# Feed-forward nets of a decoder trunk: another order of the weight chunks, two pairs of banks, loops of two steps, and reordered ends

## The reference

```python
def swiglu(x, w_gate, w_up, w_down):
    return (jax.nn.silu(x @ w_gate) * (x @ w_up)) @ w_down
...
    for l in range(DEPTH):
        x = layer_norm(ALPHA * x + 0.5 * swiglu(x, ffn1_w_gate[l], ffn1_w_up[l], ffn1_w_down[l]), ln1_g[l], ln1_b[l])
        mix = hybrid_mixer(x, w_in[l], ...)
        x = layer_norm(ALPHA * x + mix, ln2_g[l], ln2_b[l])
        x = layer_norm(ALPHA * x + 0.5 * swiglu(x, ffn2_w_gate[l], ffn2_w_up[l], ffn2_w_down[l]), ln3_g[l], ln3_b[l])
    return x
```

## Time and profile before

| | |
|---|---|
| median of 3 runs | 1083.57 us (1083.33 to 1083.84) |
| the profiled execution's own time | 1083.67 us |
| its span, first to last instruction | 1081.9 us |
| granted TensorE clock, mean over the span | 0.999 of full speed |
| busy: TensorE, its weight loads, DVE, ACT, GpSimd | 1072.1, 882.7, 772.0, 579.4, 137.3 us |
| moved by DMA | 226.39 MB, 209 GB/s over the span |

### The profile page before, as it was taken

One profiled execution on the slowest core, in us unless ns is written; L12 is line 12 of the kernel. 1 busy time (PEld: TensorE's weight loads), 2 busy tenths in 40 slices (PEclk: granted clock), 3 DMA queues, 4 the chain that ended last, 5 costly groups with the idle time before them and its releaser, 6 DMA issues.

```text
span 1081.9 us, 14282 instructions
## 1 busy us (share of the span) xinstructions
PE 1072.1 (99%) x5197; PEld 882.7 (82%) x5197; DVE 772.0 (71%) x779; ACT 579.4 (54%) x641; POOL 137.3 (13%) x137
## 2 busy tenths in 40 slices
PE   8999999999999999999999999999999999999997
PEld 6888888888888788888888888888878887888886
DVE  5756557799979775555679665677999787655566
ACT  5755654768554544444456655547774546344441
POOL 1498000000000000000006970000000000000000
PEclk9999999999999999999999999999999999999999
DMA  8877879355566486777737877775455674688761
GB/s 285 263 216 231 296 223 225 105 184 171 175 185 208 149 272 226 233 259 225 250 124 231 248 244 254 230 199 165 148 166 157 195 268 133 209 268 270 235 208 40
DMA packets 192371, 226.39 MB, mean 209 GB/s; under 512 B 31540, under 2 KB 157128, under 8 KB 192328
## 3 DMA queue, kind: packets, MB, share of 16 engines
q1 hardware_dynamic: 192328, 225.83, 65.5%
HBM read 214.26 MB, written 11.53 MB: 209 GB/s over the span
## 4 chain that ended last, share of the span: by engine, by line
PE 97%; DMA 1%; SPq 1%; DVE 1%; issue 0%; ACT 0%; DVEq 0%
PE ps L578 25%; PE ps L555 19%; PE ps L557 18%; PE ps L556 18%; PE ps L538 4%; PE ps L540 2%; PE ps L974 1%; PE ps L976 1%; PE ps L975 1%; PE ps L593 1%; DMA raw<-in_ffn_w_up 1%; PE ps L901 1%; DMA tp<-in_ln_b 0%; PE ps L686 0%; PE ps L685 0%; PE ps L684 0%
## 5 line engine op out<-in xcount | busy, mean ns | idle before, releaser
L1449 DVE TENSOR_TENSOR w_lo<-raw,w_hi 128x2048 fp32r<-128x2048 f32 x172 | 399.9, 2329 | 166.7 <-ACT w_hi L1058 165.6
L1058 ACT CAST w_hi<-raw 128x2048 fp32r<-128x2048 f32 x172 | 328.1, 1910 | 162.1 <-PE ps L578 78.9
L555 PE MATMUL ps<-w_hi,xT 128*128 128x512 f32 x848 | 331.8, 391 | 0.3 <-DVE w_lo L1461 0.2
L556 PE MATMUL ps<-w_lo,xT 128*128 128x512 f32 x848 | 330.1, 389 | 0.0
L557 PE MATMUL ps<-w_hi,xT 128*128 128x512 f32 x848 | 330.1, 389 | 0.0
L555 PEld LDWEIGHTS ps<-w_hi,xT 128*128 128x128 f32 x848 | 159.2, 188 | 36.2 <-issue 2.5
L557 PEld LDWEIGHTS ps<-w_hi,xT 128*128 128x128 f32 x848 | 159.2, 188 | 33.0
L556 PEld LDWEIGHTS ps<-w_lo,xT 128*128 128x128 f32 x848 | 159.2, 188 | 32.7
L578 PE MATMUL ps<-w_hi,rows_hi 128*128 128x512 f32 x396 | 126.6, 393 | 0.0
L578 PE MATMUL ps<-w_hi,rows_lo 128*128 128x512 f32 x396 | 125.4, 390 | 0.0
L578 PE MATMUL ps<-w_lo,rows_hi 128*128 128x512 f32 x396 | 125.2, 389 | 0.0
(11 more groups left out here) (248 smaller groups left out, 1117.1 us busy)
## 6 DMA issues: line engine op xcount, KB each, us to landing
raw<-in_ffn_w_down SPq DMA_DIRECT2D x44, 1024.0 KB, 6.6
raw<-in_ffn_w_gate SPq DMA_DIRECT2D x86, 512.0 KB, 4.1
raw<-in_ffn_w_up SPq DMA_DIRECT2D x86, 512.0 KB, 5.2
raw<-in_w_in SPq DMA_DIRECT2D x30, 1024.0 KB, 5.1
hid_dram<-qT SPq DMA_DIRECT2D x160, 64.0 KB, 2.8
qT<-hid_dram SPq DMA_DIRECT2D x40, 256.0 KB, 2.6
raw<-in_w_out SPq DMA_DIRECT2D x8, 1024.0 KB, 4.9
raw<-in_w_in SPq DMA_DIRECT2D x8, 512.0 KB, 5.0
```

Source lines behind the costliest of these rows:

```text
L555: mm(o, xT[:, c, 0, tok], h, start=c == UPPER_FIRST[0], stop=False, skip_group_check=True)
L556: mm(o, xT[:, c, 0, tok], w, start=False, stop=False, skip_group_check=True)
L1058: nc.scalar.copy(w_hi[s][:, :], raw[s][:, :]).then_inc(hi_made.sem, 1)
L1449: tt(w_lo[s][:, :], raw[s][:, :], f32(w_hi[s][:, :]), ALU.subtract).then_inc(lo_made.sem, 1)
```

## The change

- The order of a step's chunks becomes upper, the down chunk, lower, on SP, ACT, DVE and TensorE alike. Chunk 4 is thus an upper chunk (two loads, gate and up) where it was a down chunk (one load), and the down chunks from then on come one place later in the stream. The last two chunks are down chunks in both orders.
- A step with an odd number puts gate and up into banks 6 and 7, one with an even number into 4 and 5. TensorE waits ahead of an upper chunk for the hidden of the step before last, and ahead of a lower chunk for the hidden of the last step.
- TensorE's, ACT's and DVE's loops hold two steps each and run three times; steps 2, 3 and 10 stand outside TensorE's loop. SP's loops still hold one step.
- At the end of a net ACT casts chunk 32 ahead of `hidden_hi` of step 9, and DVE makes the residual of chunk 32 behind `hidden` of the last step's first tile.
- The transposes of the norm vectors go to bank 3, and `vectors` stands ahead of the first step on DVE. In `last_steps` the three last down chunks change their buffers.

```diff
@@ load_ffn (SP)
-                load(l, k0 + 4, rows(w_down, l, 0))
+                load(l, k0 + 4, gate_up(w_gate, w_up, l, 1, 512))
                 small(1)
-                def step(i):
-                    load(l, k0 + i * 3 - 1, gate_up(w_gate, w_up, l, 1, i * 256), 2)
-                    turn_hidden(l, f * (STEPS - 1) + i - 1)
-                    load(l, k0 + i * 3, gate_up(w_gate, w_up, l, 0, i * 256), 0)
-                    load(l, k0 + i * 3 + 1, rows(w_down, l, i * 256 - 256), 1)
+                def step(n):
+                    load(l, k0 + n * 3 + 2, rows(w_down, l, n * 256 - 256), 2)
+                    turn_hidden(l, f * (STEPS - 1) + n)
+                    load(l, k0 + n * 3 + 3, gate_up(w_gate, w_up, l, 0, n * 256 + 256), 0)
+                def next_upper(n):
+                    load(l, k0 + n * 3 + 4, gate_up(w_gate, w_up, l, 1, n * 256 + 512), 1)
...
@@ ffn (TensorE)
-                def step(i):
-                    pe.wait_ge(h_made.sem, h_made.at(l, s0 + i))
-                    take(l, k0 + i * 3 - 1)
-                    half(2, 1)
-                    take(l, k0 + i * 3)
-                    return half(0, 0)
-                def down(i):
-                    take(l, k0 + i * 3 + 1)
-                    pe.wait_ge(h_lo.sem, h_lo.at(l, s0 + i))
+                def upper_half(i, bank):
+                    pe.wait_ge(h_made.sem, h_made.at(l, s0 + i - 1))
+                    take(l, k0 + i * 3 - 2)
+                    half(1, 1, bank)
+                def down(n, k):
+                    take(l, k)
+                    pe.wait_ge(h_lo.sem, h_lo.at(l, s0 + n))
+                def lower_half(i, bank):
+                    pe.wait_ge(h_made.sem, h_made.at(l, s0 + i))
+                    take(l, k0 + i * 3)
+                    return half(0, 0, bank)
+                def step(i, bank, start=False):
+                    upper_half(i, bank)
+                    down(i - 1, k0 + i * 3 - 1)
+                    accumulate(2, 0, start=start).then_inc(used.sem, 1)
+                    return lower_half(i, bank)
...
-                down(1)
-                accumulate(1, 0, start=True).then_inc(used.sem, 1)
-                with pe.Fori(2, STEPS - 2 if final else STEPS - 1) as i:
-                    step(i)
-                    down(i)
-                    accumulate(1, 0).then_inc(used.sem, 1)
+                step(2, 4, True)
+                step(3, 6)
+                with pe.Fori(2, STEPS // 2) as q:
+                    step(q * 2, 4)
+                    step(q * 2 + 1, 6)
...
@@ ffn (ACT), behind the loop
+                step(STEPS - 2, 6)
                 final = l == DEPTH - 1 and f == 1
+                split(l, k0 + FFN_CHUNKS - 2)
                 if final:
-                    split_tenth(k0 + FFN_CHUNKS - 2)
+                    split_eleventh(k0 + FFN_CHUNKS - 1)
                 else:
-                    split(l, k0 + FFN_CHUNKS - 2)
+                    split(l, k0 + FFN_CHUNKS - 1)
                 hidden_hi(l, b0 + STEPS - 1, final)
-                split(l, k0 + FFN_CHUNKS - 1)
                 silu(l, s0 + STEPS, (half_used.sem, half_used.at(l, f + 1)), 4, slice(0, 1))
...
@@ ffn (DVE), ahead of the first step
+                rest(l, k0 + 4)
+                if l == 0 and f == 0:
+                    vectors()
...
@@ ffn (DVE), behind the loop
+                step(STEPS - 2, 6)
                 if late:
                     late()
                 final = l == DEPTH - 1 and f == 1
+                rest(l, k0 + FFN_CHUNKS - 2)
+                hidden_lo(l, s0 + STEPS - 1, final)
+                hidden(l, s0 + STEPS, 4, slice(0, 1))
                 if final:
-                    rest_tenth(l, k0 + FFN_CHUNKS - 2)
+                    rest_eleventh(l, k0 + FFN_CHUNKS - 1)
                 else:
-                    rest(l, k0 + FFN_CHUNKS - 2)
-                hidden_lo(l, s0 + STEPS - 1, final)
-                rest(l, k0 + FFN_CHUNKS - 1)
-                hidden(l, s0 + STEPS, 4, slice(0, 1))
+                    rest(l, k0 + FFN_CHUNKS - 1)
```

More of the change, by code:

```diff
@@ L63 @@
 for _f in FFN0:
-    for _k in [_f, _f + 1] + [_f + 3 * _i - _n for _i in range(1, STEPS) for _n in (0, 1)]:
+    for _k in [_f, _f + 1, _f + 2, _f + 3] + [_f + 3 * _i - _n for _i in range(2, STEPS) for _n in (0, 2)]:
         DMAS[_k] = 2
@@ L671, in third_of_input, with last_steps @@
                         for c in (4 + 2 * part, 5 + 2 * part):
-                            last = gate_up(w_hi[2], w_lo[2], t, c, 4 + t)
+                            last = gate_up(w_hi[2], w_lo[2], t, c, 6 + t)
                 last.then_inc(used.sem, 1)
-            def last_steps(k0, s0, step, down, turn_hidden):
+            def last_steps(k0, s0, upper, down, lower, turn_hidden):
                 def products(t, at, left, right, start=False, stop=False, bank=None):
@@ L723, in ffn, with half @@
                     gate_up_by_token(l, f, norm)
-                def half(slot, upper):
+                def half(slot, upper, bank):
                     for t in range(NT):
                         for c in range(4 * upper, 4 * upper + 4):
-                            last = gate_up(w_hi[slot], w_lo[slot], t, c, 4 + t)
+                            last = gate_up(w_hi[slot], w_lo[slot], t, c, bank + t)
                         if t == 0:
@@ L1518, in ffn, with step, next_upper @@
                 rest(l, k0 + 3)
-                def step(i):
-                    rest(l, k0 + i * 3 + 1, 1)
-                    hidden_lo(l, s0 + i)
-                    rest(l, k0 + i * 3 + 2, 2)
-                    hidden(l, s0 + 1 + i)
-                    blocks_turned(l, s0 + 1 + i)
-                    rest(l, k0 + i * 3 + 3, 0)
-                step(1)
+                rest(l, k0 + 4)
+                if l == 0 and f == 0:
+                    vectors()
+                def step(n, bank):
+                    rest(l, k0 + n * 3 + 2, 2)
+                    hidden_lo(l, s0 + n)
+                    hidden(l, s0 + 1 + n, bank)
+                    blocks_turned(l, s0 + 1 + n)
+                    rest(l, k0 + n * 3 + 3, 0)
+                def next_upper(n):
+                    rest(l, k0 + n * 3 + 4, 1)
+                step(1, 6)
+                next_upper(1)
                 if early:
                     early()
+                step(2, 4)
+                next_upper(2)
                 if second_step:
-                    step(2)
                     second_step()
-                with dve.Fori(3 if second_step else 2, STEPS - 1) as i:
-                    step(i)
+                with dve.Fori(1, STEPS // 2 - 1) as q:
+                    step(q * 2 + 1, 6)
+                    next_upper(q * 2 + 1)
+                    step(q * 2 + 2, 4)
+                    next_upper(q * 2 + 2)
+                step(STEPS - 2, 6)
                 if late:
@@ L1759, in currents @@
                 def currents():
-                    if l == 0:
-                        vectors()
                     copy(ln_cur[:, :, :], lnT[:, :, bass.ds(l, 1), :].rearrange("p n a c -> p n (a c)"))
```

90 lines of the change are left out of this document (51 added, 39 removed).

## The result

The changed kernel took 1085.83 us (median of 17 runs, 1084.99 to 1088.01), the kernel before 1083.84 us in the same runs (17, 1082.86 to 1085.57). The ratio is 1.0019, with a 95% interval of 1.0012 to 1.0026: slower by 1.3 to 2.8 us, 1.99 by the medians. 1086.2 had been forecast.

What follows compares the result with a forecast made beforehand. The prediction took TensorE, busy 99% of the span, to lose nothing between chunks, only at borders. Three ends at 0.74 (2.2 us) plus 0.3 at the start, 2.5 over 1083.67, gave 1086.2 us, range 1083.5 to 1088.5.

Steps and rivals of the forecast that it cites:

- Loops at 16.32 us, no fetch that costs: All four nets' loops: step stays 16.32 us, instruction fetches cost nothing; cost and gain 0.
- rivals 3 and 4: Loops: longer loop fetched again, 10.4 us, chance 0.05; first nets: chunk 8 holds TensorE up, 1.5 us each, chance 0.07.
- no instruction transfer stands within them: Sign for the four nets' loops in the changed kernel's trace: no instruction transfers inside, step still 16.32 us.
- Three ends at 0.74 us: Ends followed by a norm and new weights: DVE 0.74 us late, TensorE without slack; three times 0.74 is 2.2 us.
- Rival 1: At the ends: DVE's lateness is hidden, only the start's 0.3 us is left; 1084.0 us, no change; chance 0.22.
- rival 2: At the ends: tile 0's hidden, made 1.07 us earlier, shortens TensorE's waits by up to 3.3 us; 1080.4; chance 0.06.
- one of the two places named: At the ends: weight loads' waits for the normalise, or TensorE's wait ahead of its last products, grow by as much.
- The start, +0.3: Program start: chunk 4's two loads delay the norm vectors TensorE waits for; +0.3 us, ends -0.25 and +0.6.
- when the queues are drained: Start: case where the norm vectors land when queues are drained of equal bytes; cost 0.
- when they are issued: Start: case where the norm vectors land when issued, 0.5 us later; cost +0.5 us.
- A change of the order there has nothing to win: Loops: nothing is lost between chunks, waits are hidden inside the loops, so reordering gains 0.
- The sum: Whole kernel: 2.2 us at the ends plus 0.3 at the start is 2.5 us, giving 1086.2 us.

Runs made afterwards that it cites:

- e2: Kernel before with only the new order of the three ends on ACT and DVE; 1085.86 us, ratio 1.0014 to before.
- e12: Changed kernel with the old end orders on ACT and DVE, step 9's hidden in its own buffer; 1083.59 us, ratio 0.9997 to before.
- e5: Changed kernel with DVE making chunk 32's residual, then tile 0's hidden, ahead of `hidden_lo` at the ends; 1084.34 us, ratio 1.0007 to before.
- e6: Changed kernel with half of the next stage's second-chunk residual moved behind the normalisation of tile 0; 1083.52 us, ratio 0.9991 to before.
- e11: Kernel before with the second half of the next chunk's residual formed twice on DVE at each of three ends; 1088.06 us, ratio 1.0033.
- e8: Changed kernel with chunk 4's loads issued behind the norm vectors' loads in layer 0's first net; 1085.35 us, ratio 1.0006 to before.
- e9: Changed kernel with half a next-chunk residual behind tile 0's normalisation and norm vectors loaded ahead of chunk 4; 1082.86 us, ratio 0.9987 to before.
- e10: Kernel before with half a next-chunk residual behind tile 0's normalisation and norm vectors loaded ahead of chunk 4; 1084.63 us, ratio 1.0003.
- e13: Kernel before with the hidden values' turn through DRAM delayed by an extra 64 KB copy every step; 1133.33 us, ratio 1.0472.
- e14: Changed kernel with the hidden values' turn through DRAM delayed by an extra 64 KB copy every step; 1101.59 us, ratio 1.0150 to before.
- e15: Kernel before with ACT's step 2 written out ahead of its loop; 1084.24 us, ratio 1.0001.

## Why the prediction was right, and where not

- **Loops at 16.32 us, no fetch that costs:** right for the changed kernel, and rivals 3 and 4 are out: no piece of the chain between down chunks is longer, and chunk 8 holds nothing up. Its residual was ready 4.4 us before its first product, not 3.1 (51.18 and 55.60 us): the parameters' chain took 2.7 us there, not 4.5. The sign "no instruction transfer stands within them" was not met to the letter: the transfer at 82.6 us stands in the first of the loop's three passes. It cost nothing, and at the two jumps back, at about 99 and 132 us, q8 made none. The rule of the Trainium skill quoted there ("Runtime: NRT & Kernel Launch", instruction fetch mechanics) allows that if the loop lies on two pages. No run here shows on how many it lies, nor a loop that would stall by that rule.
- **Three ends at 0.74 us:** right to 0.01 us, in size, in mechanism (e2, e12) and in the claim that TensorE has no slack (e5, e6, e11). Rival 1 is out, and rival 2 also: DVE made the hidden of tile 0 1.07 us earlier, and TensorE's turn of it stayed at 0.23 us behind the last lower product in every kernel but the two with the delayed turn. The instants worked out for DVE on the clock of before (175.83, 176.46, 176.79, 179.00) are met within 0.01 us in the timeline above, when the 2.15 us are added by which the last lower product of this execution stands later. The wait came at the products just ahead of the transposes, one of the two places named. The last net cost nothing, as said: behind the third end's last lower product the changed kernel took 0.76 us more to the end of the program, and 0.74 of it is that end.
- **The start, +0.3:** wrong in size. It measured +0.04 (0.40 against 0.36 us). Of the two cases given, "when the queues are drained" was the nearer, not "when they are issued", to which I leaned. TensorE's wait there in before was also larger than the 0.24 us worked out: the product follows the transposes by 0.03 us when nothing holds it (e8), not by 0.12, which no row showed; so the wait was 0.33.
- **"A change of the order there has nothing to win":** this is the step that failed. I took eight equal steps of one execution for proof that the turn of the hidden values has room, and wrote down the room in the order of use (three chunks against four) but not what was left of it. It was 0.66 us at the least, and in other executions it runs out. For the two kernels compared this is worth little: e12 against before is 0.5 us by the medians, and its interval includes no gain at all. With the vectors' loads first (e9 against e10) it is 1.8 us, without overlap of the runs.
- **The sum:** 2.2 + 0.04 is 2.2; 1.99 was measured, 1.3 to 2.8. So the 1086.2 was right by its main term; the 0.3 of the start was an error that the measurement is too coarse to show. Whether the difference between 2.2 and 1.99 is what the chunk order gives back in an average execution stays open; the interval holds either.

## What to carry to other kernels

When an instruction is put behind one that waits longer, ask what else stands behind it on the same engine, and follow that to the next place where another engine waits; here an order changed at 175 us was paid at 190, in full. Idle time of that engine, earlier (e5) or later (e6), is where the work can go. And equal steps in one profile say that nothing was late in that execution; how near it was is the time between the producer's end and the consumer's start, step by step, and its least value is what counts.

## What was not expected of the hardware

- A stall can cost more than its own length. In e13 TensorE waited 4.13 us, and its next eight products took some 427 ns each in place of 228. The windows of that stretch (us, busy us and instructions of PE, PEld, DVE, ACT, POOL, granted clock, DMA share, GB/s) show the granted clock at 0.51, the lower of its two levels, 1.2 GHz in place of 2.4:

```profile
76.00:82.00 6.00, 6.00 (x28) 4.99 (x27) 0.60 (x1) 0.00 (x0) 5.69 (x5) 1.00 0.64 214
86.80:90.10 3.30, 3.30 (x8) 2.62 (x9) 2.52 (x2) 3.27 (x4) 3.22 (x2) 0.51 1.03 397
90.30:95.00 4.70, 4.70 (x22) 3.90 (x21) 3.90 (x3) 3.11 (x3) 4.54 (x3) 1.00 0.81 253
```

- The 1.6 us lost that way are part of why the delay cost more than the margins gave; the clock fell so behind five waits in e13, of 2.67 to 5.02 us. Stalls of 1.03 and 1.67 us, as in e10, left the pace at 228 ns. The length of the wait alone doesn't decide it: in e14 the clock fell behind a wait of 2.98 us and stayed at 1.00 behind one of 3.32.
- Which activation table was loaded when the loop was entered decided here whether its body loaded tables in every pass: 34 loads of 1283 ns in before, 4 in the changed kernel, for one step written out. That is 39 us of ACT's time, and it lay in ACT's idle time: without the loads e15 took as long as before, 1.0001 (0.9992 to 1.0010).
